# Hybrid decoder block with expert retrieval: down products of 32 dense tokens by gathered rows, candidate sums in one operation

## The reference

```python
    q = (ht @ w_query).reshape(N, PEER_HEADS, 2, PEER_QDIM // 2)
    s1 = jnp.einsum('nhd,kd->nhk', q[:, :, 0], sub_keys_1)
    s2 = jnp.einsum('nhd,kd->nhk', q[:, :, 1], sub_keys_2)
    t1, i1 = lax.top_k(s1, PEER_TOPK)
    t2, i2 = lax.top_k(s2, PEER_TOPK)
    cand = (t1[..., :, None] + t2[..., None, :]).reshape(N, PEER_HEADS, PEER_TOPK * PEER_TOPK)
    cidx = (i1[..., :, None] * N_KEYS + i2[..., None, :]).reshape(N, PEER_HEADS, PEER_TOPK * PEER_TOPK)
    sc, pos = lax.top_k(cand, PEER_TOPK)
    eidx = jnp.take_along_axis(cidx, pos, axis=-1)
    gate = jax.nn.softmax(sc.astype(jnp.float32), axis=-1).astype(h.dtype)
...
        u = expert_down[e_c]
        a = jax.nn.gelu(jnp.einsum('cd,chkd->chk', x_c, u), approximate=False)
        vv = expert_up[e_c]
        return jnp.einsum('chk,chkd->cd', g_c * a, vv)
```

## Time and profile before

| | |
|---|---|
| median of 3 runs | 1531.55 us (1530.72 to 1532.54) |
| profiled execution: span from first to last instruction | 1528.9 us |
| TensorE busy | 1507.2 us, 99% |
| VectorE busy | 1229.5 us, 80% |
| ScalarE busy | 626.8 us, 41% |
| POOL (GpSimd) busy | 534.0 us, 35% |
| DMA | 378.85 MB, mean 248 GB/s |
| granted TensorE clock | 0.999 of full speed |

### The profile page before, as it was taken

How to read it: one execution, slowest core, us unless ns; L and a number is a source line. 1 busy time by engine, 2 the same in 40 slices (tenths; PEclk the granted TensorE clock), 3 DMA queues, 4 the chain that set the end, 5 groups by cost and what they waited for, 6 DMA issues and landing times.

```text
span 1528.9 us, 22605 instructions
## 1 busy us (share of the span) xinstructions
PE 1507.2 (99%) x8475; PEld 1344.2 (88%) x8475; DVE 1229.5 (80%) x2265; ACT 626.8 (41%) x1050; POOL 534.0 (35%) x357
## 2 busy tenths in 40 slices
PE   9999999999999999999999999999999999999997
PEld 6888888888899999998888888999999999999996
DVE  5577875449999999975676777888888889888885
ACT  6247565342222356662333333333333333333335
POOL 0323002055746710002111112555555556555530
PEclk9999999999999999999999999999999999999999
DMA  7302003323313568889899989999999999999971
GB/s 309 147 30 83 1 1 128 111 86 122 132 57 116 171 197 310 316 315 365 289 312 299 309 296 341 364 366 371 357 358 371 363 374 362 364 365 357 369 256 69
DMA packets 148509, 378.85 MB, mean 248 GB/s; under 512 B 11793, under 2 KB 76689, under 8 KB 145457
## 3 DMA queue, kind: packets, MB, share of 16 engines
q1 hardware_dynamic: 100400, 201.74, 38.1%
q0 software_dynamic: 37200, 138.56, 24.7%
q10 hardware_dynamic: 10800, 37.11, 6.6%
HBM read 338.50 MB, written 38.86 MB: 247 GB/s over the span
## 4 chain that ended last, share of the span: by engine, by line
PE 85%; DVE 10%; DMA 2%; ACT 1%; issue 1%; SPq 0%; ACTq 0%; DVEq 0%
PE bank L1900 22%; PE bank L1805 20%; PE bank L1524 12%; PE bank L1906 11%; PE bank L1814 10%; PE bank L1737 2%; DVE oh L1406 2%; DVE gp L1414 2%; DVE gp L1411 2%; DVE oh L1409 2%; PE bank L1721 1%; PE bank L1643 1%; DVE d_lo L1395 1%; DMA w_raw<-wts 1%; PE bank L1823 1%; PE bank L1641 1%
## 5 line engine op out<-in xcount | busy, mean ns | idle before, releaser
L1805 PE MATMUL bank<-h_hi,d_hi 128*128 128x384 f32 x1024 | 349.2, 341 | 1.1 <-DVE h_lo L1260 1.1
L1805 PE MATMUL bank<-h_lo,d_hi 128*128 128x384 f32 x1024 | 345.0, 337 | 0.0
L581 POOL DMA_INDIRECT p_in<-rows,p_row x128 | 160.2, 1251 | 404.1 <-DVE p_dot L1433 186.0
L581 POOL DMA_INDIRECT p_in<-up,p_row x128 | 172.0, 1344 | 190.7 <-DVE p_dot L1433 96.3
L1814 PE MATMUL bank<-h_hi,d_lo 128*128 128x384 f32 x1024 | 200.2, 338 | 0.0
L1805 PEld LDWEIGHTS bank<-h_hi,d_hi 128*128 128x128 f32 x1024 | 192.5, 188 | 4.0 <-issue 1.3
L1805 PEld LDWEIGHTS bank<-h_lo,d_hi 128*128 128x128 f32 x1024 | 192.4, 188 | 3.2
L1900 PE MATMUL bank<-u_hi,w_hi_e 128*128 128x512 f32 x750 | 192.3, 392 | 0.3 <-DVE w_lo_e L1458 0.3
L1900 PE MATMUL bank<-u_hi,w_lo_e 128*128 128x512 f32 x750 | 191.0, 390 | 0.0
L1906 PE MATMUL bank<-u_lo,w_hi_e 128*128 128x512 f32 x750 | 190.8, 390 | 0.0
L1814 PEld LDWEIGHTS bank<-h_hi,d_lo 128*128 128x128 f32 x1024 | 180.9, 188 | 0.0
(11 more groups left out here) (292 smaller groups left out, 2454.4 us busy)
## 6 DMA issues: line engine op xcount, KB each, us to landing
d_raw<-down SPq DMA_DIRECT2D x128, 512.0 KB, 5.8
u_raw<-up SPq DMA_DIRECT2D x128, 512.0 KB, 6.4
gates_dram<-ev ACTq DMA_DIRECT2D x12, 2048.0 KB, 6.8
g_e<-gates_dram SPq DMA_DIRECT2D x32, 768.0 KB, 9.8
w_raw<-wts SPq DMA_DIRECT2D x9, 2048.0 KB, 8.2
act_dram<-f_act ACTq DMA_DIRECT2D x59, 192.0 KB, 3.9
a_e<-act_dram SPq DMA_DIRECT2D x59, 192.0 KB, 5.8
xt<-x_in SPq DMA_DIRECT2D x2, 2048.0 KB, 11.8
```

What stands on the lines that cost most here:

```text
L581: pool.indirect_dma_start(out=p_in[n % GR][:], out_offset=None, in_=rows if kind == "D" else up.rearrange("n p d -> (n p) d"), in_offset=b ...
L1805: nc.tensor.matmul(bank[6 + e % 2][:, 0:TD], d_hi[e % DH_R][:, k], h[:, k, 0:TD], start=(k == j == 0), stop=False)
```

## The change

32 tokens of the third block (`XT`, the last 32 of the 384) stay dense for the gates and the `up` products, but their down products are no longer part of the score blocks: these have 352 columns (`TN`). Their 32 x 128 rows of `down` are gathered instead, 32 gathers (`XP`) of 128 rows each, with 4 x 32 partitions holding the same 32 tokens. The tokens' row is copied four times to `x_h`, the row numbers to `e_row`, by small DMAs on SyncE. VectorE makes 32 dots, four in each of groups 0 to 7 of the gate stage; ScalarE applies gelu and moves the results back to the 32 tokens. They are multiplied into the gate weights ahead of the last group, transposed by TensorE behind group 9, and split in three bf16 parts, so that the last group takes three products and 96 matmuls. In the main loop the gelus of these 32 columns are 1 (a memset by POOL), and the product is written to `w_e`, which shares its place with `w_lo_e`; so it waits until TensorE is done with expert e - 3.

`early_to` now gives three score blocks to each of groups 0 to 7 and two to the others: `E_LAST` goes from 55 to 69 and `NE` from 59 to 73. In the gate stage `d_lo` of the first block of each group stays with VectorE, and the others go to POOL, in one queue with the gathers. The candidate sums of the four token blocks are one operation, and the three semaphores of `top16` are one. Not shown: the places in SBUF, the widths of stored and loaded gelus (`TN`), semaphore counts that follow, and the copy of the block's gates to `x_w`.

```diff
+XT = 32
+XG = P // XT
+XP = PICKS // XG
+TN = TD - XT
+XGRP = NTG - XT // TG
+X_GROUPS = 8
+X_GELU = X_GROUPS
+
+
 E_AHEAD = 2
 E_REST = 2 * PH + E_AHEAD
 E_SLOTS = 33
 E_DVE = E_SLOTS + 2
 E_GATES = E_SLOTS + 4
+EARLY_BUSY = 3
...
-    return E_GATES + (3 * i + 1) // 2
+    return E_GATES + EARLY_BUSY * min(i, X_GROUPS) + 2 * max(0, i - X_GROUPS)
+
+
+def pool_low(f):
+
+    if f < E_DVE:
+        return True
+    firsts = [E_DVE] + [early_to(i) for i in range(NTG + 1)] + [E_LAST + 2]
+    return f < NE and f not in firsts
+
+
+def pool_lows(f):
+
+    return sum(pool_low(i) for i in range(f + 1))
+
+
+def dve_lows(f):
+
+    return sum(not pool_low(i) for i in range(f + 1))
...
-E_UP = early_to(NTG - 3)
+E_UP = early_to(NTG - 2)
...
+def x_first(i):
+
+    return XP // X_GROUPS * min(i, X_GROUPS)
...
+            sp.wait_ge(S("xs_done"), TDB)
+            for g in range(XG):
+                sp.dma_start(x_h[g * XT:(g + 1) * XT], xs[P - XT:, TDB - 1]).then_inc(S("x_moved"), 16)
...
-                    sp.wait_ge(S("w_done"), e - 3)
-                sp.dma_start(a_e[e % 4][:], act_dram[e]).then_inc(S(f"a_loaded{e % 4}"), 16)
+                    sp.wait_ge(S("w_mul"), e - 3)
+                sp.dma_start(a_e[e % 4][:, 0:TN], act_dram[e]).then_inc(S(f"a_loaded{e % 4}"), 16)
...
+                if f == E_SLOTS + DR - 1:
+                    sp.wait_ge(S("x_picked"), 2)
+                    for g in range(XG - 1):
+                        sp.dma_start(e_row[g * XT:(g + 1) * XT], x_row[P - XT:, g * XP:(g + 1) * XP])\
+                          .then_inc(S("x_moved"), 16)
                 if f == E_UP:
 
-                    sp.wait_ge(S("oh_done"), 1)
+                    sp.wait_ge(S("x_used"), XP)
...
+            def gather(n):
+
+                if n == 0:
+                    pool.wait_ge(S("x_picked"), 2)
+                    pool.wait_ge(S("x_moved"), 16 * (2 * XG - 1))
+                if n >= 4:
+                    pool.wait_ge(S("x_used"), n - 3)
+                pool.indirect_dma_start(
+                    out=e_in[n % 4][:], out_offset=None, in_=rows,
+                    in_offset=bass.IndirectOffsetOnAxis(ap=e_row[:, n:n + 1], axis=0)).then_inc(S(f"p_loaded{n % 4}"), 16)
+
+            for i in range(NTG):
+                if i == 0:
+                    for n in range(4):
+                        gather(n)
+                for f in range(early_to(i - 1) if i else E_DVE, early_to(i)):
+                    if pool_low(f):
+                        early_low(f)
+                for n in range(x_first(i) + 4, min(XP, x_first(i + 1) + 4)):
+                    gather(n)
+            for f in range(early_to(NTG - 1), NE):
+                if pool_low(f):
+                    early_low(f)
+
             pool.wait_ge(S("rows_ready"), 1)
-            pool.wait_ge(S("gate_mm"), NTG * (TG // PSTEP))
+            pool.wait_ge(S("gate_mm"), GATE_MMS)
+            for i in range(4):
+                nc.gpsimd.memset(a_e[i][:, TN:], 1.0).then_inc(S("pool_set"), 1)
...
+                if i == X_GELU:
+                    last = slice(P - XT, P)
+                    act.wait_ge(S("x_used"), XP)
+                    nc.scalar.activation(e_act[0:P - XT], e_dot[0:P - XT], ACT.Gelu).then_inc(S("x_gelu"), 1)
+                    nc.scalar.activation(x_act[last, PICKS - XP:], e_dot[last], ACT.Gelu).then_inc(S("x_gelu"), 1)
+                    act.wait_ge(S("x_gelu"), 1)
+                    for g in range(XG - 1):
+                        act.dma_start(x_act[last, g * XP:(g + 1) * XP], e_act[g * XT:(g + 1) * XT])\
+                           .then_inc(S("x_moved"), 16)
...
+                link(V.tensor_tensor(cand[:], tv[r][0][:].unsqueeze(3).broadcast_to([P, TB, TOPK, TOPK]),
+                                     tv[r][1][:].unsqueeze(2).broadcast_to([P, TB, TOPK, TOPK]), ALU.add))
...
+            dve.wait_ge(S("key_done"), 2 * PH)
+            V.scalar_tensor_tensor(x_row[extra], x_of(key[0]), float(NK), x_of(key[1]), ALU.mult, ALU.add)\
+             .then_inc(S("x_picked"), 1)
+            V.scalar_tensor_tensor(e_row[extra], x_of(key[0])[:, PICKS - XP:], float(NK), x_of(key[1])[:, PICKS - XP:],
+                                   ALU.mult, ALU.add).then_inc(S("x_picked"), 1)
+            link(V.memset(x_act[:], 0.0))
...
+            def dot(n):
+
+                dve.wait_ge(S(f"p_loaded{n % 4}"), 16 * (n // 4 + 1))
+                V.tensor_tensor_reduce(out=e_in[n % 4][:], in0=e_in[n % 4][:], in1=x_h[:], scale=1.0, scalar=0.0,
+                                       op0=ALU.mult, op1=ALU.add, accum_out=e_dot[:, n:n + 1])\
+                 .then_inc(S("x_used"), 1)
+
+            def gated():
+
+                dve.wait_ge(S("x_gelu"), 2)
+                dve.wait_ge(S("x_moved"), 16 * (3 * XG - 2))
+                V.tensor_tensor(x_w[:], x_w[:], x_act[:], ALU.mult)\
+                 .then_inc(S("x_picked"), 1)
+
+            def three_parts():
+
+                dve.wait_ge(S("slot_ps"), 4)
+                w_t = bank[0][:, P - XT:P]
+                link(V.tensor_copy(sl_w[0][:], w_t))
+                link(V.tensor_tensor(sl_r[:], w_t, sl_w[0][:], ALU.subtract))
+                link(V.tensor_copy(sl_w[1][:], sl_r[:]))
+                link(V.tensor_tensor(sl_w[2][:], sl_r[:], sl_w[1][:], ALU.subtract))
+
+            def one_hots_extra(i, lows):
+                r = i % 2
+                dve.wait_ge(S("gate_mm"), (i - 1) * (TG // PSTEP))
+                tok = slice(i * TG, (i + 1) * TG)
+                wide = lambda t: t.rearrange("p (q l) -> p q l", l=TL).unsqueeze(2).broadcast_to([P, TG // TL, NK, TL])
+                iota = iota_k[:].unsqueeze(1).broadcast_to([P, TG // TL, NK, TL])
+                parts = [wide(t[:, i * TG - TN:(i + 1) * TG - TN]) for t in sl_w]
+                V.tensor_tensor(oh[r][0][:], iota, wide(sl_key[0][:, tok]), ALU.is_equal).then_inc(S("oh_a"), 1)
+                for f in lows:
+                    d_low(f)
+                V.tensor_tensor(oh_b[r][1][:], iota, wide(sl_key[1][:, tok]), ALU.is_equal)
+                dve.wait_ge(S("oh_a"), i + 1)
+                V.tensor_tensor(gp_b[r][0][:], oh[r][0][:], parts[0], ALU.mult)
+                link(V.tensor_tensor(gp_b[r][1][:], oh[r][0][:], parts[1], ALU.mult))
+                V.tensor_tensor(oh_b[r][0][:], oh[r][0][:], parts[2], ALU.mult).then_inc(S("oh_done"), 1)
...
-            one_hots(0, range(E_DVE, E_GATES))
-            for i in range(1, NTG):
-                one_hots(i, range(early_to(i - 1), early_to(i)))
+            for i in range(NTG):
+                if i == XGRP:
+                    three_parts()
+                lows = [f for f in range(early_to(i - 1) if i else E_DVE, early_to(i)) if not pool_low(f)]
+                if i < XGRP:
+                    one_hots(i, lows)
+                else:
+                    one_hots_extra(i, lows)
+                for n in range(x_first(i), x_first(i + 1)):
+                    dot(n)
+                if i == X_GELU + 1:
+                    gated()
             for f in range(early_to(NTG - 1), NE):
-                d_low(f)
+                if not pool_low(f):
+                    d_low(f)
...
-                V.tensor_tensor(a_v, a_v, g_e[n % 3][:, :, e % GB], ALU.mult).then_inc(S("w_mul"), 1)
+                if e == 0:
+                    dve.wait_ge(S("pool_set"), 26)
+                if e >= 3:
+                    dve.wait_ge(S("pu_done"), e - 2)
+                V.tensor_tensor(w_e[e % 3][:].rearrange("p (i t) -> p i t", t=TG),
+                                a_e[e % 4][:].rearrange("p (i t) -> p i t", t=TG), g_e[n % 3][:, :, e % GB],
+                                ALU.mult).then_inc(S("w_mul"), 1)
...
-                        nc.tensor.matmul(bank[6 + e % 2][:, 0:TD], d_hi[e % DH_R][:, k], h[:, k, 0:TD],
+                        nc.tensor.matmul(bank[6 + e % 2][:, 0:TN], d_hi[e % DH_R][:, k], h[:, k, 0:TN],
...
-                if e < E_DVE:
-                    pe.wait_ge(S("f_lo_done"), e + 1)
+                if pool_low(e):
+                    pe.wait_ge(S("f_lo_done"), pool_lows(e))
                 else:
-                    pe.wait_ge(S("d_lo_done"), e - E_DVE + 1)
+                    pe.wait_ge(S("d_lo_done"), dve_lows(e))
...
+                        one, parts = (oh[r][1], gp[r]) if i < XGRP else (oh_b[r][1], gp_b[r] + [oh_b[r][0]])
+                        for j, part in enumerate(parts):
                             m = nc.tensor.matmul(bank[2 + q % 4][:, tt * NK:(tt + 1) * NK],
-                                                 oh[r][1][:, t // TL, :, t % TL], gp[r][j][:, t // TL, :, t % TL],
-                                                 start=(j == 0), stop=(j == 1))
+                                                 one[:, t // TL, :, t % TL], part[:, t // TL, :, t % TL],
+                                                 start=(j == 0), stop=(j == len(parts) - 1))
                     m.then_inc(S("gate_mm"), 1)
```

(3 more changed lines are left out.)

100 lines of the change are left out of this document (63 added, 37 removed).

## The result

The changed kernel takes 1560.74 us (median of 4 runs, 1558.18 to 1562.98), the kernel before 1531.32 beside it: ratio 1.019, 95% interval 1.0176 to 1.0205. The profiled execution has a span of 1559.5 us against 1528.9.

The account below looks back on a forecast made before the run. Bounds: TensorE and VectorE in the search, VectorE in the gate stage, TensorE in the main loop. Terms -6 + 80.2 + 57.1 - 95.2 - 0.6 = +35.5 took the span from 1528.9 to 1564.4; forecast 1567 us, range 1508 to 1600.

Parts of the forecast that it names:

- Block price: Score blocks on TensorE: 352 columns instead of 384 bring a block from 4.16 to 3.84 us, 0.32 less.
- Part 1: Up to the first one-hots: shorter blocks and merged candidate sums let VectorE be ready at 554 instead of 560.1, -6 us.
- Part 2: Gate stage: dots, and moved d_lo costing VectorE 2.2 us each through turns with POOL; 222.2 us instead of 142.0, +80.2.
- Part 3: Early main loop: 72 experts instead of 58 at 4.08 us each, +57.1 us; the product's new wait costs nothing.
- Part 4: Late main loop: 53 periods instead of 67, 51 at 8.8 us and two at 8.04, -95.2 us.
- B: Rival, late main loop: DMA at its limit, 365 GB/s, 9.47 us a period; 1601 us; chance 0.11.
- C: Rival, gate stage: POOL runs beside the 16-bit operations, TensorE bounds it, late loop as forecast; 1531 us, no change; chance 0.20.
- D: Rival, gate stage and late loop: POOL takes no turns, late period falls to VectorE's own 8.4 us; 1511 us; chance 0.14.
- E: Rival, gate stage costs more: bf16 at half pace, gathers held up, or matmuls not shortening; 1575 to 1600 us; chance 0.09.

Follow-up runs that it names:

- merged-only kernel: The kernel before with the candidate sums of the four token blocks in one operation and nothing else: 1532.0 us, ratio 1.0005.
- runs with memsets: The changed kernel with each POOL subtraction from block 35 on replaced by a memset of the same tile: 1540.09 us in one run.
- best of these kernels: The changed kernel with all d_lo from block 35 on VectorE, picks 9 per 10 experts, and the 2 MB gate stores issued by POOL: 1516.66 us, ratio 0.9910.

## Why the prediction was right, and where a term was off

**Block price.** 0.32 us less was right in the gate stage (steps of 3.84 us); in the late loop TensorE's own period is 7.97, not 8.04.

**Part 1, -6 us: failed, -0.9.** The term that failed is VectorE's gain in the search: 8 us forecast, about 3 measured. The candidate sums did lose 5.2 us of busy time (22.8 to 17.6; I had 7), and the row numbers cost the 0.6 I gave them. What I left out is that the waiting for POOL is not tied to the candidate sums: POOL's subtractions take their turns from whatever VectorE runs at that time. The merged-only kernel shows another limit just as near, ScalarE's queue.

**Part 2, +80.2: right, +83.3.** 18.9 us of sum, 19.2 taken, 18.87 measured; both halves of it (POOL's turns on 16-bit operands, and the dots at 1.14) are shown by the runs with memsets and with VectorE's own `d_lo`. The bf16 operations, at the 16-bit pace, came as costed. The eight periods took 2.6 us less than costed, what lies behind them 5.7 more. Of that 2.3 are the last group's 96 matmuls, 8.11 us where 5.8 was costed at full clock. TensorE had waited 5.5 us ahead of them, and the granted clock behind that wait was 0.50, the level of 1.2 GHz (columns as in rows 2):

```profile
753.00:757.00 4.00, 3.71 (x35) 3.71 (x36) 1.37 (x2) 1.20 (x2) 0.00 (x0) 0.50 0.00 0
```

The gating took 3.8 us where 0.3 was allowed (1.8 of waiting for its input, and a product of 1.99 beside POOL's subtraction), the small operations of the three parts 2.6 instead of 0.9 (a 128x32 cast of 1.92 instead of 0.2, again beside POOL's), and group 10, which met no subtraction of POOL, gave 2.2 back. The gathers delayed nobody in this kernel, though one issue takes 1.91 us there on the median instead of 1.02. The rule of the Trainium skill that was weighed (SBUF — State Buffer, "Who interferes with whom") is borne out: the loser does fully block, whatever its type. The same section says that an operation of GpSimd that only writes does not contend; the memset run agrees.

**Part 3, +57.1: right.** 72 x 4.08; the product's new wait cost nothing.

**Part 4, -95.2: the size was off, -108.2.** I took 8.8 us for each of 51 periods and 8.04 for two, 8.77 on the mean; measured are 8.53. The mis-sized term is the DMA's: it sustains 399 GB/s, 1.5% more than the 393 I took, and it moved 3.40 MB a period (399 GB/s x 8.53 us), not 3.46. VectorE's sum of 8.4 was near the truth (8.31 busy); I had raised the period to 8.8 for a DMA limit that lies lower. What I had not seen is that the time is not simply the larger of the two: VectorE's work goes on top of the interruptions by late loads. How much each contributes was not separated. The tail came as costed, 0.3 us less than before.

**The sum.** +5 in the first part, +3 in the second, -13 in the late loop: -5 of 1564.4, which is the measured span of 1559.5. So the total is closer than its terms, since 8 us too little and 13 too much stand against each other; that part of the agreement is luck.

**The rivals.** B (365 GB/s as the ceiling) is refuted: 399 over 400 us in the changed kernel, 399 also with the schedule alone. The Trainium skill (DMA: Bandwidth & Descriptors, "Where 436 GB/s comes from") puts the HBM limit per core near 358, as half of what a stack gives two cores; this kernel runs on one core, and the measurement of 399 decides against that limit here. C and D need a POOL without turns; there is none. But D's late loop, at VectorE's 8.4, lies nearer to the measured 8.53 than my 8.8, and a kernel on D's side exists: with VectorE's own `d_lo` and the picks spread otherwise the same change is 0.6% faster. Of E nothing came true but longer issues of the gathers, which cost nothing: the bf16 operations kept their pace and the matmuls shortened.

**What stays open.** The best of these kernels gains 14.5 us of the 24 that shorter blocks alone are worth in the old schedule. Which part of the remaining 10 is the last group of the gate stage and which the late loop at 400 GB/s was not separated. Nor was VectorE's share in the late loop's surplus from the DMA's: every edit that relieved one relieved the other. Why single loads of `down` take 29 us in the full late loop was not tried either.
